# Six weight slots and six load stages in the gate/up part of a decoder layer, and gelu as ScalarE's last step of a chunk

## The reference

```python
def conv_glu_ffn(h, w_gate, w_up, conv_w, conv_b, w_down):
    g = h @ w_gate                                   # 256x2048 @ 2048x8192
    u = h @ w_up
    gp = jnp.pad(g, ((0, 0), (CONV_WIDTH - 1, 0), (0, 0)))
    g = conv_b + gp[:, 0:S] * conv_w[0]
    for j in range(1, CONV_WIDTH):
        g = g + gp[:, j:j + S] * conv_w[j]
    return (jax.nn.gelu(g, approximate=True) * u) @ w_down   # 256x8192 @ 8192x2048
...
    h = rms_norm(x, ffn_pre_g[l])
    y = conv_glu_ffn(h, w_gate[l], w_up[l], conv_w[l], conv_b[l], w_down[l])
    x = x + rms_norm(y, ffn_post_g[l])
```

## Time and profile before

| what | value |
|---|---|
| median of 3 runs | 1432.68 us |
| the profiled execution | 1432.29 us, span 1430.5 us |
| PE / PEld / DVE / ACT / POOL busy | 1413.1 / 1170.6 / 1239.6 / 822.3 / 359.3 us |
| granted TensorE clock | 0.998 |
| HBM read | 273.67 MB, 193 GB/s over the span |

### The profile page before, as it was taken

One profiled execution on the slowest core, in us unless ns is written; L12 is line 12 of the kernel. 1 busy time (PEld: TensorE's weight loads), 2 busy tenths in 40 slices (PEclk: granted clock), 3 DMA queues, 4 the chain that ended last, 5 costly groups with the idle time before them and its releaser, 6 DMA issues.

```text
span 1430.5 us, 18897 instructions
## 1 busy us (share of the span) xinstructions
PE 1413.1 (99%) x6502; PEld 1170.6 (82%) x6502; DVE 1239.6 (87%) x1867; ACT 822.3 (57%) x1082; POOL 359.3 (25%) x609
## 2 busy tenths in 40 slices
PE   9999999999999999999999999999999999999997
PEld 9888888888878788877888888888787888888886
DVE  6857678965586899999999999999998999999997
ACT  7455545554574655665655655655655666766663
POOL 0701020720003224443324443234443000000000
PEclk9999999999999999999999999999999999999999
DMA  8765666555666667767667767677768666666662
GB/s 267 219 186 154 193 189 187 166 163 178 176 186 207 211 214 227 235 208 225 211 215 230 235 210 226 213 222 220 235 209 266 196 200 214 197 207 208 204 214 96
DMA packets 149706, 293.75 MB, mean 205 GB/s; under 512 B 17232, under 2 KB 30832, under 8 KB 149360
## 3 DMA queue, kind: packets, MB, share of 16 engines
q1 hardware_dynamic: 132416, 274.71, 61.1%
q0 software_dynamic: 16384, 16.81, 4.3%
q10 hardware_dynamic: 816, 1.09, 0.2%
HBM read 273.67 MB, written 2.10 MB: 193 GB/s over the span
## 4 chain that ended last, share of the span: by engine, by line
PE 54%; DVE 26%; DMA 13%; issue 4%; ACT 2%; SPq 1%; DVEq 0%; POOL 0%; ACTq 0%; POOLq 0%
PE psum L2092 17%; DMA stage<-in_w_up 13%; DVE w_lo L1572 11%; PE psum L1865 7%; PE psum L1869 7%; PE psum L1867 7%; PE psum L1832 3%; DVE scratch L1583 2%; PE psum L2073 2%; PE psum L2074 2%; PE psum L2075 2%; DVE act_g L1470 2%; PE psum L1836 2%; DVE factors L1590 2%; DVE factors L1596 2%
## 5 line engine op out<-in xcount | busy, mean ns | idle before, releaser
L2092 PE MATMUL psum<-w_hi,hT 128*128 128x512 f32 x2112 | 575.3, 389 | 4.3 <-DVE w_lo L1572 4.1
L2092 PEld LDWEIGHTS psum<-w_hi,hT 128*128 128x128 f32 x2112 | 395.5, 188 | 90.2 <-issue 8.3
L906 ACT CAST w_hi<-stage 128x1024 fp32r<-128x1024 f32 (+1 forms) x326 | 312.9, 989 | 228.4 <-DMA stage<-in_w_up 132.8
L1572 DVE TENSOR_TENSOR w_lo<-stage,w_hi 128x1024 fp32r<-128x1024 f32 (+1 forms) x326 | 365.2, 1145 | 46.3 <-ACT w_hi L906 46.1
L2092 PE MATMUL psum<-w_lo,hT 128*128 128x512 f32 x1056 | 325.2, 389 | 0.0
L1104 DVE TENSOR_TENSOR w_lo<-stage,w_hi 128x1024 fp32r<-128x1024 f32 x141 | 175.6, 1250 | 89.6 <-ACT w_hi L638 88.6
L638 ACT CAST w_hi<-stage 128x1024 fp32r<-128x1024 f32 x141 | 147.8, 1050 | 179.4 <-PE psum L1869 143.0
L2092 PEld LDWEIGHTS psum<-w_lo,hT 128*128 128x128 f32 x1056 | 198.2, 188 | 41.3
L1076 POOL DMA_DIRECT2D gate_rows_f<-gate_T x256 | 135.2, 537 | 377.2 <-DVE gate_T L1451 323.2
L1076 POOL DMA_DIRECT2D up_rows_f<-up_T x256 | 135.0, 536 | 48.7 <-DVE up_T L1451 39.7
L1865 PE MATMUL psum<-w_hi,hT 128*128 128x512 f32 x312 | 124.9, 400 | 0.0
(11 more groups left out here) (227 smaller groups left out, 2071.7 us busy)
## 6 DMA issues: line engine op xcount, KB each, us to landing
stage<-in_w_gate SPq DMA_DIRECT2D x128, 512.0 KB, 4.1
stage<-in_w_up SPq DMA_DIRECT2D x128, 512.0 KB, 5.1
stage<-in_w_qkv SPq DMA_DIRECT2D x93, 512.0 KB, 3.8
stage<-in_w_down SPq DMA_DIRECT2D x86, 512.0 KB, 4.7
stage_wide<-in_w_down SPq DMA_DIRECT2D x42, 512.0 KB, 4.7
stage<-in_w_o SPq DMA_DIRECT2D x32, 512.0 KB, 3.9
gate_rows_f<-gate_T POOLq DMA_DIRECT2D x256, 32.0 KB, 3.8
up_rows_f<-up_T POOLq DMA_DIRECT2D x256, 32.0 KB, 3.6
```

Of the source, the lines that this page charges most:

```text
L906: nc.scalar.copy(w_hi[slot_of[v]][:, 0:width], src).then_inc(s_hi, 1)
L1572: nc.vector.tensor_tensor(w_lo[slot_of[v]][:, 0:width], src, w_hi[slot_of[v]][:, 0:width].bitcast(F32), ALU.subtract).then_inc(s_lo, 1)
L2092: ins = nc.tensor.matmul(c_bank(G, t, c), a[:, j, ROWS[t]], w[slot_of[v]][:, COLS[c]], start=(q == 0 and j == 0 and n == 0), stop=False, s ...
```

## The change

It adds two slots and two stages to gate/up. The two slots (`w_hi_early0/1`) lie at 56 and 48 KiB of the arena, where `aT` keeps the gated rows of chunks 14, 15 and 12, 13: so one is taken out of the turn before G = 12, the other before G = 14, and from chunk 12 on `gated_rows` also waits for the last block of the chunk before. The two stages lie in `ffn_g`; they leave the turn at the fourth block of down, and `ffn_g` is loaded after its 16th block, when both have been read. Gelu moves from ACT's step 14 to its step 15.

```diff
+EARLY_SLOTS, EARLY_STAGES = (SLOTS, SLOTS + 1), (STAGES, STAGES + 1)
+RETIRED_AT = (14, 12)
...
+        ffn_g_at = (nc.sbuf_base + 31) // 32 * 32
         ffn_g = sb("ffn_g", [P, D])
+        stage_early = nc.alloc_sbuf_tensor_at("stage_early", [P, len(EARLY_STAGES) * UNIT], F32, offset=ffn_g_at)
...
+        for s in range(len(EARLY_SLOTS)):
+            w_hi.append(place(f"w_hi_early{s}", [P, UNIT], F32R, at=(56 - 8 * s) * KIB))
+            w_lo.append(place(f"w_lo_early{s}", [P, UNIT], F32R))
...
-        CONV_AT, GATED_AT, ACT_GELU_AT = (10, 11, 13), 15, 14
+        CONV_AT, GATED_AT, ACT_GELU_AT = (10, 11, 13), 15, 15
...
-        in_turn = [(s, BASE - RING + s + 1) for s in range(RING)]
+        in_turn = [(s, 0) for s in EARLY_SLOTS] + [(s, BASE - RING + s + 1) for s in range(RING)]
         for g in range(len(blocks)):
+            for s, G in zip(EARLY_SLOTS, RETIRED_AT):
+                if blocks[g] == (G, 0):
+                    in_turn = [turn for turn in in_turn if turn[0] != s]
...
-        stages_in_turn = [(s, s - RING) for s in range(RING)]
+        stages_in_turn = [(s, None) for s in EARLY_STAGES] + [(s, s - RING) for s in range(RING)]
...
             if u == 2 * (D0 + WIDE_STAGE_FROM):
-                stages_in_turn = [(s, None) for s in range(RING, STAGES)] + stages_in_turn
+                EARLY_LEFT = [before for s, before in stages_in_turn if s in EARLY_STAGES]
+                stages_in_turn = ([(s, None) for s in range(RING, STAGES)]
+                                  + [turn for turn in stages_in_turn if turn[0] not in EARLY_STAGES])
...
             load_ffn(0)
-            sp.dma_start(ffn_g[:, :], ffn_post_g.to_broadcast((P, D))).then_inc(s_ffn_g, 16)
...
             for g, (G, q) in enumerate(blocks):
+                if g == D0 + PAIRS // 2:
+                    for u in EARLY_LEFT:
+                        sp.wait_ge(s_lo, unit_taken(u))
+                    sp.dma_start(ffn_g[:, :], ffn_post_g.to_broadcast((P, D))).then_inc(s_ffn_g, 16)
...
                 if slot_free[v]:
                     act.wait_ge(s_used, slot_free[v])
+                elif slot_of[v] in EARLY_SLOTS:
+                    act.wait_ge(s_resid, resid_done(OUT_CHUNKS - 1, TT - 1))
                 else:
                     act.wait_ge(s_a_out, F_ITERS)
...
                 dve.wait_ge(s_gelu, i + 1)
+                if i >= min(RETIRED_AT):
+                    dve.wait_ge(s_used, block_used(LASTS[i - 1]))
```

More of the change, by code:

```diff
@@ L138, in layer_kernel @@
         h_sums = nc.alloc_sbuf_tensor_at("h_sums", [P, len(F_SUMMED), 2, 2, SEQ], F32R, offset=post_at)
+        ffn_g_at = (nc.sbuf_base + 31) // 32 * 32
         ffn_g = sb("ffn_g", [P, D])
+        stage_early = nc.alloc_sbuf_tensor_at("stage_early", [P, len(EARLY_STAGES) * UNIT], F32, offset=ffn_g_at)
+        stage += [stage_early[:, s * UNIT:(s + 1) * UNIT] for s in range(len(EARLY_STAGES))]
         cols = sb("cols", [P, 3 * KT])
@@ L292, in layer_kernel @@
         s_ffn_g = sem("ffn_gain_rows_loaded")
-        s_stage = [sem(f"stage_full{s}") for s in range(STAGES)]
+        s_stage = [sem(f"stage_full{s}") for s in range(STAGES + len(EARLY_STAGES))]
         s_hi = sem("w_hi_ready")
@@ L463, in layer_kernel @@
         stage_of, stage_before, loads_of = [], [], []
-        stages_in_turn = [(s, s - RING) for s in range(RING)]
-        loads = [BASE // RING] * RING + [0] * (STAGES - RING)
+        stages_in_turn = [(s, None) for s in EARLY_STAGES] + [(s, s - RING) for s in range(RING)]
+        loads = [BASE // RING] * RING + [0] * (STAGES - RING + len(EARLY_STAGES))
         for u in range(2 * len(blocks)):
             if u == 2 * (D0 + WIDE_STAGE_FROM):
-                stages_in_turn = [(s, None) for s in range(RING, STAGES)] + stages_in_turn
+                EARLY_LEFT = [before for s, before in stages_in_turn if s in EARLY_STAGES]
+                stages_in_turn = ([(s, None) for s in range(RING, STAGES)]
+                                  + [turn for turn in stages_in_turn if turn[0] not in EARLY_STAGES])
             s, before = stages_in_turn.pop(0)
@@ L482, in pair_stage @@
             s = stage_of[2 * g]
+            if s >= STAGES:
+                return stage_early[:, :]
             return (stage_all[:, s * UNIT:(s + 2) * UNIT] if s < RING
@@ L593, in _ @@
             load_ffn(0)
-            sp.dma_start(ffn_g[:, :], ffn_post_g.to_broadcast((P, D))).then_inc(s_ffn_g, 16)
             def wait_for_unit(u):
                 if stage_before[u] is None:
-                    sp.wait_ge(s_used, block_used(D0 - 1))
+                    if stage_of[u] < STAGES:
+                        sp.wait_ge(s_used, block_used(D0 - 1))
                 else:
```

## The result

The changed kernel takes 1419.09 us (median of four runs, 1418.95 to 1419.57), the kernel before 1432.81 (four runs, 1432.63 to 1433.73). The interval is about 2.5 us wide to each side, so the times alone do not tell 13.7 from 11.4; what follows rests on the traces.

A forecast was written before the change was run, and what follows sets the result against it. PE follows a late DVE in gate/up, losing 12.4 us; less 0.4 at G = 14 and 0.6 for small holes gives 11.4, so 1432.29 becomes 1420.9, plus 0.4 for the median: 1421.3. Range of 8 in 10: 1419.8 to 1427.5.

The forecast's parts named there:

- What bounds it: In gate/up PE follows DVE, which comes late; 12.4 us is all that slots and stages can give back.
- DVE's slack of 1.85 us: Per gate/up chunk: DVE's work is 40.33 us against PE's 42.18, so 1.85 us are to spare.
- Six stages: Gate/up loads go out three blocks ahead, so DVE's idle 1.04 and 0.59 us a chunk go.
- Six slots: Gate/up: four slots alone cost DVE 0.7 to 1.1 us a chunk; with six, or five, PE is not starved.
- Gelu: Gate/up, ACT's step 15: DVE's idle 0.93 us for unit 15's cast goes; gelu's 1.06 us is hidden.
- G = 14: Last chunk, four slots: the 1.17 us hole at down's start goes with 1.4 to spare; 0.4 left in.
- The gain row: Its 1 MB load in down, between blocks 15 and 16, is hidden: nothing; a stall would cost up to 3 us.
- the other waits: `gated_rows` from chunk 12 on and ACT's wait for `s_resid`: both already met, costing nothing.
- the bound: Low end of the forecast time, 1419.9 us: all 12.4 back, and the runs' 0.4 not added.
- small holes in the other 14 chunks: Gate/up outside G = 14: 0.6 us taken off the gain for holes that remain.
- half the gain: Rival: 2.2 us of new DVE waits a gate/up chunk cost 0.35 each, 5.3 in all, 1426.6 us; chance 0.16.
- The moves between partitions: Rival: POOL's gate/up moves land late beside earlier loads; at 9.2 us landing, 16 us lost, 1437; chance 0.05.

The follow-up runs named there:

- the held version: The changed kernel with SyncE loading the gain row twice in down, waiting for each, before block 16's loads; 1419.05 us, ratio 0.9901.

## Why the prediction missed its range

- **What bounds it: right.** PE followed DVE. But 12.76 us were to be had in gate/up where I read 12.4: 2790 matmuls take 632.40 us, 0.22667 each, and the 0.2268 that I read from one row of 144 makes 632.8 of it.
- **DVE's slack of 1.85 us: right in kind, too small.** It is 2.30 in a chunk without other waits. The trace before gave 1.85 because its three waits, and some too short to be marked, also cost DVE 0.08 of overlap each, which I counted as work. That the wait at the adding of rows is 1.86 on average (24.2 / 13) is luck: it is nine times 2.30, and less in four chunks with a late cast.
- **Six stages: right** that the load waits go, from 111.6 to 9.2 us. "That is the loss" was too much: alone the stages take back 4.9 of PE's 12.8.
- **Six slots: no gain beside the other two parts, as counted, but for the wrong size.** Four slots cost DVE 2.05 us a chunk, not 0.7 to 1.1; I counted only the splits of summed blocks and missed unit 11's cast behind the first tap. That 2.05 still ends in time, by a hair. With five slots it is not the same as with six, as I had said: DVE idles 1.44 us, inside its slack.
- **Gelu: right and under-rated.** I listed its 0.93 us as one of three waits of a chunk. Taking it away alone gave 9.6 us, more than either of the other parts alone.
- **G = 14: right** that the hole of 1.17 goes. The gelu step is what closes it (it is back at 1.1 with gelu at 14).
- **The gain row, the other waits: right,** nothing. PE does lose 0.5 us near down's block 16, but it lost as much there before.
- **The step that failed is the sum, and in it the bound.** "12.4 us is all that the slots and stages of gate/up can give back" was worth 12.76; the change in down and ahead of gate/up, put at nothing, was 0.47 - 0.13 = 0.34; and the bound took the median to lie on its profile, where it lies 0.10 below. 0.37 + 0.34 + 0.10 are the 0.8 us by which 1419.9 was too high. The middle of the forecast was too high by more, because I also kept back 0.4 us at G = 14 and 0.6 for "small holes in the other 14 chunks", with no row behind either; both measured 0. The account of 1421.3 - 1419.1 = 2.2: 1.0 for holes that I kept back, 0.37 for the pace, 0.34 for down and the start, 0.49 for the offset (I added 0.4; after the change the median lies 0.1 below its profile). The bound of 1419.8 was thus no bound of the mechanism, only of my reading of one run.
- **Down's 0.47** is not settled: PE's loss from down's first matmul to its last is 1.5 us before, 1.1 and 1.4 after in two profiles, 1.0 and 1.3 with four slots. It varies as much as it gained, so part of the miss is chance.
- **The rivals** fell: half the gain needed 2.2 us of new waits a chunk in addition to the work, and no chunk of the changed kernel has more than 1.5, but for G = 14 with 2.1. The moves between partitions landed in at most 5.3 us (5.6 before) beside a longer load queue:

```profile
DMA to landing us min/median/max: 1.7/3.6/5.3
```

The chip's part of that rival, slower landing, is not seen in the changed kernel; its effect on the tap is. In two chunks the tap waited for the moves, which it did in none of these 13 chunks before; DVE's slack took it up. With gelu back at step 14, or with DVE's slack used up by more work, the same wait made a hole. What is late is POOL, not the landing. Its first move of a chunk goes out 1.6 us after DVE starts to turn the gate rows (785.49 after 783.90), but 4.3 us after it in G = 4 (619.58 after 615.26) and as much in G = 11. The same 2.7 us of delay stand in the same two chunks of all 14 traces, that of the kernel before among them, so the change did not make it; it brought ACT to the tap earlier. The profile names no wait for it; why POOL is late stays open.

## What to carry to other kernels

When an engine is late by less than it idles, add up its idle time over one period and compare it with its slack: any cut that brings the sum under the slack gives the whole gain, and what is cut beyond that gives nothing. So the worth of a part depends on the others. Here any two of three parts gave most of the gain; the cheapest, one instruction moved by one place, gave 9.6 us alone and 1.7 us of PE's time as the last of the three, and the 16 KB a partition of slots gave nothing once the other two were in. Try the pairs before paying memory for all. Once the slack argument closes, keep nothing back in the sum without a row, and let the low bound be open by the spread of the runs.

## What the runs showed of the hardware

Two 1 MB loads of the same row, one after the other, took 8.1 and 4.8 us to land: the first went out when three weight loads of 512 KB were still on their way, the second with nothing else queued by SP. The windows over 1136 to 1150 us (length, busy PE, PEld, DVE, ACT, POOL, PEclk, DMA share, GB/s), of the changed kernel, where the row and the next weight loads run together:

```profile
1136.00:1150.00 14.00, 14.00 (x63) 11.58 (x63) 14.00 (x21) 7.08 (x9) 0.00 (x0) 1.00 0.85 301
```

and of the held version, where SP issues only the rows from 1137.1 us on:

```profile
1136.00:1150.00 14.00, 14.00 (x64) 11.58 (x63) 14.00 (x22) 7.08 (x9) 0.00 (x0) 1.00 0.69 262
```

DVE and PE are busy 14.00 of 14.00 us in both: 39 GB/s more or less beside them change nothing. A load's time to land told more of what was queued beside it than of its size.

POOL, which issues 32 small moves in each chunk, was 2.7 us late in G = 4 and G = 11 of every trace, whatever the slots and stages were. They are seven chunks apart, 224 moves. The cause is not shown. POOL's timeline of the changed kernel, G = 4 and then G = 8:

```profile
619.58 8.41 POOL L1097 DMA_DIRECT2D gate_rows_f<-gate_T  x16 [26.43 <-issue]
...
785.49 8.41 POOL L1097 DMA_DIRECT2D gate_rows_f<-gate_T  x16 [20.97 <-DVE gate_T L1472]
```
